# Attention: reciprocal ahead of the next maximum; ctx's output product, norm and queries moved into the opening of the first expert layer

## The reference, cut to what matters

```python
for l in range(DEPTH):
    h = modulate(rms_norm(x, norm1_g[l]), mod[0], mod[1])       # hc the same, of xc
    y, yc = mixer(h, hc)                                        # yc in layer 0 alone
    x = x + mod[2] * y
    h2 = modulate(rms_norm(x, norm2_g[l]), mod[3], mod[4])
    x = x + mod[5] * peer_ffn(h2, ...)
    # layer 0: the same three lines for xc, with modc
# layer 0: yc = concat([attend(qc, kc, vc), conformer_conv(cuc, ...)]) @ w_out
# peer_ffn, for each head: s = q @ sub_keys; the 16 best of 16 + 16; e = their experts
#   act = gelu(sum(x * u[e])); y += softmax(top)[e] * act * v[e]
```

## Time and profile before

| | |
|---|---|
| median of 3 executions | 2536.29 us |
| the profiled execution | 2532.21 us, of which the span of the trace is 2530.2 us |
| busy in the span | PE 77%, DVE 66%, ACT 46%, POOL 35% |
| gathers | 768 (512 in layer 0, 256 in layer 1), 128 rows of 8 KB each: 1.049 MB |
| DMA over the span | 952.22 MB, mean 376 GB/s |
| granted TensorE clock, mean | 0.862 of 2.4 GHz |

### The profile page before, as it was taken

How to read it: one execution, slowest core, us unless ns; L and a number is a source line. 1 busy time by engine, 2 the same in 40 slices (tenths; PEclk the granted TensorE clock), 3 DMA queues, 4 the chain that set the end, 5 groups by cost and what they waited for, 6 DMA issues and landing times. The chain is left out here.

```text
span 2530.2 us, 31698 instructions
## 1 busy us (share of the span) xinstructions
PE 1956.2 (77%) x10844; PEld 935.4 (37%) x10844; DVE 1671.2 (66%) x4157; ACT 1159.4 (46%) x3156; POOL 891.4 (35%) x808
## 2 busy tenths in 40 slices
PE   8999877888786767777877776799997776666765
PEld 5667432443341212333333331478752221122110
DVE  1634589887667667767576867473557666666665
ACT  2342456776635444544453544412335444444444
POOL 0001334544334444444344444100114444444442
PEclk9989898888898878888989998899998877788675
DMA  9554999999999999999999999895169999999997
GB/s 369 206 192 131 411 424 418 422 403 409 425 425 427 426 425 426 426 425 426 422 416 426 426 426 427 295 373 175 73 247 412 426 426 427 426 426 427 427 427 308
DMA packets 146418, 952.22 MB, mean 376 GB/s; under 512 B 16464, under 2 KB 22096, under 8 KB 44752
## 3 DMA queue, kind: packets, MB, share of 16 engines
q0 software_dynamic: 113472, 847.30, 80.2%
q1 hardware_dynamic: 32784, 102.89, 11.1%
HBM read 949.07 MB, written 1.05 MB: 376 GB/s over the span
## 5 line engine op out<-in xcount | busy, mean ns | idle before, releaser
L1080 PE MATMUL pY<-uv,diag 64*64 64x512 f32 x6144 | 992.5, 740 | 504.7 <-ACT diag L1156 485.7
L961 POOL DMA_INDIRECT uv<-uv_dram,idx x768 | 866.5, 1128 | 1270.8 <-PE pY L1080 1027.3
L1314 DVE SCALAR_TENSOR_TENSOR uv<-uv,H 128x1024 f32<-128x1024 f32 x768 | 939.7, 1224 | 535.3 <-DMA uv<-uv_dram,idx 520.6
L1080 PEld LDWEIGHTS pY<-uv,diag 64*64 64x64 f32 x6144 | 194.2, 151 | 1132.9 <-ACT diag L1156 990.2
L1148 ACT ACTIVATE gelu<-dots 128x1 f32<-128x1 f32 x768 | 154.8, 202 | 859.4 <-DVE uv L1314 839.7
L1156 ACT ACTIVATE diag<-cst,coef 128x128 f32<-128x128 f32 x768 | 308.3, 401 | 72.1 <-ACT coef L1152 1.9
L1152 ACT ACTIVATE coef<-gelu,gate 128x1 f32<-128x1 f32 x768 | 226.3, 295 | 28.1 <-issue 0.4
L984 PE MATMUL pqs<-hT,wring 128*128 128x256 f32 x512 | 126.8, 404 | 0.7 <-ACT S L1131 0.7
L984 PEld LDWEIGHTS pqs<-hT,wring 128*128 128x128 f32 x512 | 100.6, 202 | 45.3 <-issue 31.5
L134 PE MATMUL plh<-hT,wring 128*128 128x256 f32 (+1 forms) x512 | 106.3, 368 | 3.7 <-PEq L78 3.3
L1148 ACT ACT_TABLE_LOAD x79 | 101.4, 1283 | 1.4
(11 more groups left out here) (448 smaller groups left out, 2225.3 us busy)
## 6 DMA issues: line engine op xcount, KB each, us to landing
aw<-ada_w_dram POOLq DMA_DIRECT2D x12, 2048.0 KB, 9.6
wring<-peer_q_dram SPq DMA_DIRECT2D x36, 512.0 KB, 13.5
uv<-uv_dram,idx POOLq DMA_INDIRECT x768
wring<-hg_zz_dram SPq DMA_DIRECT2D x20, 512.0 KB, 4.9
wring<-w_in_dram SPq DMA_DIRECT2D x16, 512.0 KB, 10.1
arena<-hg_zz_dram SPq DMA_DIRECT2D x16, 512.0 KB
arena<-ada_w_dram POOLq DMA_DIRECT2D x4, 2048.0 KB
h_aw<-ada_w_dram POOLq DMA_DIRECT2D x4, 2048.0 KB
```

The costliest lines, as they stand in the source:

```text
L961: nc.gpsimd.indirect_dma_start(out=uv[:, n % SLOTS, :], out_offset=None, in_=t[f"uv{l}"], in_offset=bass.IndirectOffsetOnAxis(ap=idx[:, s ...
L1080: last = nc.tensor.matmul(pY[crossed(own, half), b, half * 512:(half + 1) * 512], diag[own, n % DIAGS, own], uv[own, n % SLOTS, D + half * ...
L1314: v.scalar_tensor_tensor(out=uv[:, j, 0:D], in0=uv[:, j, 0:D], scalar=1.0, in1=H2[:, own, :], op0=ALU.mult, op1=ALU.mult, accum_out=dots[: ...
```

## The change

Four edits that belong together.

1. In the context attention, DVE takes the reciprocal of unit u-2 ahead of the maximum of u, not behind the taps; of the taps, 3 lie beside an even unit and 9 beside an odd one (6 and 6 before).
2. The front phase ends after the attention, the convolution and the modulation groups: group 14 moves to loop step u = 16, group 15 behind the transposes of the attention's output. The product with `w_out`, the residual, the norm and the affine of the context leave it. The ring has four w_out tiles, not eight.
3. The opening of `peer_phase(0)` is `ContextOutput`: for block 0 (128 tokens) output product, norm, queries, scores and `topk(0)`; three of block 1's product tiles beside the norm, the rest beside the selection; block 1's norm and queries after it. `topk(1)` and `topk(2)` move beside the picks of step 0, two parts for each pick, and head 1's queries ahead of picks 1 and 3. The last four w_out tiles are loaded into gather buffers 6 and 7 at the phase's start, and gather 6 waits for `b1_out`.
4. The target's first two weight loads (`rest_load`, into `H2`) are issued when block 1's sum of squares is done, ahead of `weights(2)` and `weights(3)`.

```diff
@@ -99,7 +99,7 @@
...
-        lin = [("w_in", 12), ("w_in", 4), ("w_out", 8), ("peer_q0", 16), ("peer_q0", 16),
+        lin = [("w_in", 12), ("w_in", 4), ("w_out", RING), ("peer_q0", 16), ("peer_q0", 16),
@@ -338,9 +342,7 @@
...
-            for i in range(KT):
-                load_tile(sp, "w_out", i, first[2] + i)
-            lin_ahead(sp, 2)
+            lin_ahead(sp, 1)
@@ -511,7 +507,7 @@
...
-                if u < len(UNITS) and u % 2 == 0:
+                if u % 2 == 0:
                     modulate(6 + u // 2)
@@ -534,24 +530,9 @@
...
-            for i in range(2):
-                tile(2, i, range(4))
-            for i in range(2, 4):
-                tile(2, i, range(4))
-            for i in range(4):
-                tile(2, i, range(4, KT))
-            for i in range(4, KT):
-                tile(2, i, whole)
-            for k in range(KT):
-                if k == 6:
-                    modulate(14)
-                pe.wait_ge(r_sq, k + 1)
-                last = mm(A[0][:, 0:T], ones[:], h1[:, k, :], start=(k == 0), stop=(k == KT - 1))
-            last.then_inc(r_sum, 1)
             modulate(15)
             turn(14)
             turn(15)
-            keep_warm(nc, po[:], cst, 4)
@@ -662,7 +643,7 @@
...
-                if u < len(UNITS) and u % 2 == 1:
+                if u % 2 == 1:
                     take_rows(6 + u // 2)
@@ -676,22 +657,11 @@
...
+            take_rows(15)
...
-            act.wait_ge(acc_ready, first[2])
-            for k in range(KT):
-                act.wait_ge(r_out, k + 1)
-                a.activation(h1[:, k, :], xT[:, k, CX], ACT.Square).then_inc(r_sq, 1)
-            take_rows(14)
-            act.wait_ge(r_rs, 1)
-            a.activation(rs[:, XX], rs[:, XX], ACT.Sqrt).then_inc(r_root, 1)
-            take_rows(15)
-            act.wait_ge(m_fin, 5)
-            for k in range(0, KT, 2):
-                act.wait_ge(r_y, k + 1)
-                a.activation(hT[:, k, CX], hT[:, k, CX], ACT.Identity, scale=gainT[:, 0, 1, k, 1:2], bias=modT[:, 0, 3, k, 1:2])
@@ -709,6 +679,7 @@
...
+            TAPS_BESIDE = (3, 9)
@@ -761,19 +732,19 @@
                                        in1=lat_rs[:, k // 2, :], op0=ALU.mult, op1=ALU.mult).then_inc(l_rs, 1)
             taps(60)
             for u in range(len(UNITS) + 2):
+                if u >= 2:
+                    w = u - 2
+                    dve.wait_ge(at["exp"], w + 1)
+                    if w >= 2:
+                        dve.wait_ge(at["norm"], w - 1)
+                    v.reciprocal(mx[:, 6 + w % 2:7 + w % 2], mx[:, 4 + w % 2:5 + w % 2]).then_inc(at["rd"], 1)
                 if u < len(UNITS):
                     x = u % 2
                     dve.wait_ge(at["s"], u + 1)
                     if u >= 2:
                         dve.wait_ge(at["nmx"], u - 1)
                     v.reduce_max(mx[:, x:x + 1], A[x][:, 0:T], AX).then_inc(at["mx"], 1)
-                    taps(6)
-                if u >= 2:
-                    w = u - 2
-                    dve.wait_ge(at["exp"], w + 1)
-                    if w >= 2:
-                        dve.wait_ge(at["norm"], w - 1)
-                    v.reciprocal(mx[:, 6 + w % 2:7 + w % 2], mx[:, 4 + w % 2:5 + w % 2]).then_inc(at["rd"], 1)
+                    taps(TAPS_BESIDE[x])
@@ -782,39 +753,14 @@
...
-            dve.wait_ge(m_turned, 14)
-            dve.wait_ge(at["norm"], len(UNITS))
-            mod_finish(fin, 0, (2, 3, 4, 5), pc[:, 32:96].rearrange("p (n c) -> p n c", c=2))
             dve.wait_ge(c_root, 1)
             v.reciprocal(rs[:, CX], rs[:, CX]).then_inc(c_step, 1)
...
-            def outputs(p):
-
...
-            for p in range(4):
-                outputs(p)
-            dve.wait_ge(r_sum, 1)
-            v.tensor_scalar(rs[:, XX], A[0][:, 0:T], 1.0 / D, EPS, ALU.mult, ALU.add).then_inc(r_rs, 1)
...
-            dve.wait_ge(r_y, KT)
-            for k in range(1, KT, 2):
-                own = hT[:, k, CX]
-                v.tensor_scalar(own, own, gainT[:, 0, 1, k, 1:2], modT[:, 0, 3, k, 1:2], ALU.mult, ALU.add)
             dve.wait_ge(m_turned, GROUPS)
+            mod_finish(fin, 0, (2, 3, 4, 5), pc[:, 32:96].rearrange("p (n c) -> p n c", c=2))
@@ -920,15 +858,15 @@
...
+            opening.sync_late(sp)
...
+            opening.sync_queries(sp)
+            if l == 0:
+                sides[0].sync_first(sp)
@@ -953,7 +891,7 @@
...
-                if opening and n == SLOTS - 2:
+                if n == SLOTS - 2:
                     pool.wait_ge(opening.b1_out, 1)
@@ -1006,59 +944,19 @@
...
+            opening.tensor(pe)
             pe.wait_ge(rows_copied, 2 * BLOCKS)
-            keep_warm(nc, pY[:, 1, 0:512], cst, 9 if l == 0 else 3)
+            keep_warm(nc, pY[:, 1, 0:512], cst, 3)
...
-                if opening and n in (1, 3):
+                if n in (1, 3):
                     queries(1, n // 2)
-                if opening and n == 6:
+                if n == 6:
...
+                if n == 6:
...
-                    if (b, k) == ((1, 2) if late else (0, 9 if opening and s == 0 else 4)):
+                    if (b, k) == ((1, 2) if late else (0, 9 if s == 0 else 4)):
                         queries(h + HEADS_AHEAD, 0)
@@ -1288,13 +1160,10 @@
...
+            opening.vector(dve)
+            for part in range(TOPK):
+                topk(0, part)
+            opening.second(dve)
             inverse(0)
             gates(0)
@@ -1828,6 +1697,225 @@
...
+class ContextOutput:
+
+    BESIDE = 3
...
+    def bank(self, n):
+
+        return self.pY[:, n % 4 // 2, n % 2 * 512 + n // 4 * P:n % 2 * 512 + (n // 4 + 1) * P]
+
+    def sync_late(self, sp):
+
+        for i in range(RING, KT):
+            sp.dma_start(self.late[:, i - RING, :], self.t["w_out"][i]).then_inc(self.late_loaded, 16)
+
+    def sync_queries(self, sp):
+
+        for i in range(RING):
+            self.load_tile(sp, "peer_q0", i, self.q_first + i)
...
+        def products(b, tiles):
+
+            for i in tiles:
+                n, g = KT * b + i, self.out_first + i
+                if i < RING:
+                    pe.wait_ge(self.w_loaded[g % RING], 16 * (g // RING + 1))
+                    w = self.wring[:, g % RING, :]
+                else:
+                    pe.wait_ge(self.late_loaded, 16 * RING)
+                    w = self.late[:, i - RING, :]
+                if n >= 4:
+                    pe.wait_ge(self.x, n - 3)
+                for k in range(KT):
+                    last = mm(self.bank(n), w[:, k * P:(k + 1) * P], self.mixc[:, k, self.cols(b)], start=(k == 0), stop=(k == KT - 1))
+                last.then_inc(self.product, 1)
+                if b == 1 and i < RING:
+                    pe.wait_ge(self.product, n + 1)
+                    pe.sem_inc(self.acc_ready, 1)
+            if b == 1 and KT - 1 in tiles:
+                pe.wait_ge(self.product, 2 * KT)
+                pe.sem_inc(self.b1_out, 1)
...
+        def sums(b):
+
+            for k in range(KT):
+                pe.wait_ge(self.squared, KT * b + k + 1)
+                last = mm(self.b[b][:, 0:P], self.ones[:], self.sq[b][:, k, :], start=(k == 0), stop=(k == KT - 1))
+            last.then_inc(self.summed, 1)
...
+        def rows(b):
+
+            if b == 0:
+                pe.wait_ge(self.x, 2 * KT)
+            for k in range(KT):
+                last = nc.tensor.transpose(self.pY[:, b, k * P:(k + 1) * P], self.hT[:, k, self.cols(b)], self.ident)
+            last.then_inc(self.t_done, 1)
+
+        products(0, range(KT))
+        sums(0)
+        products(1, range(self.BESIDE))
+        queries(0, self.pq)
+        scores(0)
+        products(1, range(self.BESIDE, KT))
+        rows(0)
+        sums(1)
+        queries(1, self.pt)
+        rows(1)
+        scores(1)
+
...
+        affine(0)
+        queries(0, self.pq[:, :, 0:P])
+        scores(0)
+        act.wait_ge(self.table, 1)
+        squares(1)
+        rows(0)
+        exponentials(0)
+        root(1)
+        affine(1)
+        queries(1, self.pt)
+        rows(1)
+        scores(1)
...
+    def vector(self, dve):
+
+        self.residual(dve, 0, range(KT))
+        self.norm(dve, 0)
+        self.residual(dve, 1, range(self.BESIDE))
+
+    def second(self, dve):
+
+        self.residual(dve, 1, range(self.BESIDE, KT))
+        dve.wait_ge(self.x, 2 * KT)
+        dve.sem_inc(self.acc_free, RING)
...
+    def sync_first(self, sp):
+
+        sp.wait_ge(self.opening.summed, 2)
+        for i in range(2):
+            self.rest_load(sp, i)
```

More of the change, by code:

```diff
@@ L405, in tile @@
                         pe.wait_ge(n_ha, 4 + k + 1)
[L406 to L411, removed]
+                    rhs = (h1[:, k, :], Kx[:, k, :])[seq]
                     last = mm(pl[g // 2 % 2][:, i % 2, :], wring[:, g % RING, k * P:(k + 1) * P], rhs,
-                              start=(k == 0 and (i % 2 == 0 or not (seq == 2 and i < 4))), stop=(k == KT - 1),
-                              skip_group_check=True)
```

(59 more changed lines are left out.)

180 lines of the change are left out of this document (110 added, 70 removed).

## The result

| | before | after |
|---|---|---|
| median of 5 executions | 2534.53 us | 2522.59 us |
| ratio, 95% interval | | 0.9945 (0.993 to 0.9961) |
| the profiled execution, span of its trace | 2532.2 us, 2530.2 | 2522.6 us, 2520.8 |
| gather 0 starts | 243.71 | 213.00 |
| mean GB/s in the 100 us from gather 0 | 403 | 372 |

A forecast was written before the change was run, and what follows sets the result against it. Gathers run at the DMA ceiling, so gather 0's start bounds the front. 14 us from the attention and 16 from the half-width opening bring it 30.1 earlier; less 1.5, 2536.3 - 28.6 = 2507.7 us, range 2502 to 2512, wider 2501 to 2517.

The forecast's parts named there:

- its 14 us: Context attention: reciprocal ahead of the maximum shortens four pairs of units from 40.88 to 26.8 us, gain 14, bounds 9.5 and 14.5.
- dips of the clock: Rival, attention: PE's lower-clock dips stay, gain 10 in place of 14, time 2511.7 us; chance 0.13.
- its 15.0 where 1.5 stood: Opening, block 0's output product: 64 matmuls take 15.0 us, plus 1.5 for the pause ahead of it, up to 3.
- that rival: Block 1's norm: a drain at two table switches puts gather 8 off by 2.8 us more, time 2510.5; chance 0.02.
- part 4: After gather 0: picks leave one or two gathers queued; between 0.5 us more filled and 6 more idle, 1.5 taken.
- change nothing at the end: all lie beside gathers: Earlier H2 loads, reordered head-1 queries and layer 1's later modulation were claimed to cost nothing at the end.
- the second rival: Opening at the lower clock: half of block 0's product and queries slow, gather 0 8 us later, 2516; chance 0.08.
- the third, the picks starve the gathers: After gather 0: gather 8 later, PE full from pick 1 to 40, 5 to 8 us idle, 2511 to 2515; chance 0.09.
- The announced sign: Prediction wrong if gather 0 lies past 220 or the window behind it falls under 385 GB/s; 395 to 405 expected.

The follow-up runs named there:

- the tiles ahead: Changed kernel with the target's w_in tiles 2 and 3 loaded behind the first two, 4 to 7 at least eight picks ahead, not four: 2509.72 us, again 2508.14.
- a pause of 7.99 us: Against the tiles ahead: nine 512-column matmuls added on PE ahead of tile 2 at pick 11; 2512.48 us, ratio to before 0.9913.

## Why the prediction was wrong, point by point

- **Direction and start: right.** The attention gives about its 14 us (edit 1 alone: 12.5 at gather 0, 15.2 by the medians), with no dips of the clock. Gather 0 was worked out at 213.6; the three traces of the changed kernel have it at 213.0, 214.6 and 216.0. The product took 2.2 us over its 15.0 where 1.5 stood, all in its first half. The table switch in block 1's norm reads `ACT_TABLE_LOAD` 1.28 us at 219.53 and its activation at 220.83, so the rule weighed in the prediction (the Trainium skill, "ScalarE: Activation LUTs", section "What ACT_TABLE_LOAD costs") has no drain to show here either, and that rival is out.
- **The step that failed is part 4**, "I take 1.5", the term for what comes back after gather 0, between 0.5 us more filled and 6 more idle. It measured 12.3 us in the profiled execution by gather 100 (8.5 and 12.1 in the other two traces; 9.3 to 10.1 in all three by gather 80). Its layout was right: gather 12 was at +36.6 where +36 was worked out, gather 16 at +46.3 where +45 was. It said itself that the engines would then run with one or two gathers queued. What was missing was any wait of PE behind gather 16.
- **Why it was missing.** A side tile was priced by its matmuls alone, and its load as so many bytes. The only landing time that was read was that of loads on quiet queues, 3.6 to 4.1 us; none was read beside running gathers and behind other loads. There the same 512 KB took 18.2 us, and the mixer asks four picks ahead: 10 us at 2.46 each, 8.4 at PE's 2.1. The sentence on the earlier loads, the moved queries and the modulation, "change nothing at the end: all lie beside gathers", was the error in words: it asks whether the DMA engines have room, and not whether PE will wait. The trace of before had the sign. Its first tile landed late too, and PE stood longer than in after:

```profile
268.87 2.08 PE L1924 MATMUL side<-arena,H 128*128 128x256 f32 x4 [9.21 <-DMA H<-w_in_dram]
```

  It cost nothing there (1.4 us lost in gathers 10 to 20), because before had picked 0 to 2 within 16 us of gather 0 and gathers 8 to 10 stood in the queue. In the new order these picks are done only at +29, and the wait that hurts, now the one for the third tile, comes at +53 to +59. What decides is the reserve, the work already given to the DMA engines when PE stops (at 259.66 before, at 266.11 after). How long they stay full, and what they move then:

```profile
259.66:281.66 22.00, 12.79 (x54) 7.27 (x55) 11.60 (x29) 6.11 (x21) 5.00 (x4) 0.69 1.01 425
281.66:289.66 8.00, 8.00 (x49) 3.25 (x47) 5.20 (x14) 3.26 (x8) 3.80 (x4) 1.00 0.94 354
```
```profile
266.11:276.11 10.00, 4.04 (x13) 1.60 (x13) 6.37 (x14) 7.31 (x17) 1.76 (x1) 0.69 1.01 423
276.11:286.11 10.00, 10.00 (x53) 5.94 (x53) 5.23 (x17) 4.85 (x14) 3.68 (x3) 0.96 0.58 193
```

  They stay at the ceiling for 22 us in before (one gather, issued at 273.16, came in between) and for 10 in after. The shorter wait meets the smaller reserve, and is dear.
- **The second term** was the 5 us without work on PE while block 1 is normed: the second rival names these 5 us but prices the lower clock for block 0 alone, and part 4 has no term for it. It cost block 1's queries 2.4 us, which with a late tile behind them became 4.3 us of time.
- **The rival that came true** is the third, the picks starve the gathers, with its place right, its mechanism (low clock) a half, and its price, 5 to 8 us idle, too small. The announced sign held: a window under 385 GB/s was named as what would make the prediction wrong, and it was 372.
- **The sum with the step mended** is 2509.72 and 2508.14 us, where 2507.7 stood. That is not the kernel that was predicted, but against before beside it the gain is 25.8 and 26.6 us where 28.6 stood, so the other terms add up to within 3 us. Of the 12 to 15 us that were missing, some 10 are the late tiles together with the clock. The rest, 2 to 5 us, is a gather 0 that came 0.7 to 2.4 us later than worked out in six of the ten traces with this start, and losses behind gather 80 and between the layers. These differ between traces of one kernel by more than they matter (lead at the last gather 8.5, 17.2 and 9.8 us) and stay open. That edit 1 alone gave 2520.28 and all four 2519.59 beside it says the same from the other side: as it stands the new opening brings next to nothing, and with the tiles ahead another 10.6.

## What to carry to other kernels

When work is moved closer to running gathers, price each load that it waits for by its landing there, with what stands ahead of it in its own queue, and not by bytes or by loads on quiet queues. Both tiles that came late were issued within 5 us behind the query tiles of the next head; the others, asked for just as many picks ahead, came in time. Ask of each wait of the old trace not how long it is but how much reserve stands in front of it: a stop of 9.2 us was free where the DMA engines stayed full for 22 us, and a pause of 7.99 us where they stayed full for 10 cost 5.9 us of DMA time. An expected idle stretch of PE has a second price, the lower clock of the work that follows it.

## What was not expected of the hardware

One 512 KB load took 3.6 to 4.1 us from issue to landing with little else in flight, and 18.2 us when it was issued at 253.81. That is near the 19.7 us that eight gathers take, but eight gathers were not in flight: POOL had issued gather 13 at 251.67, and by 253.81 their queue had moved 13.08 MB, 12.5 of the fourteen gathers of 1.049 MB issued by then. What stood ahead of the load was in its own queue: a `keys` tile of 128 KB and two query tiles of 512 KB, issued from 252.48 on. They landed 8.9, 11.7 and 15.0 us after their issue, at 261.4, 264.6 and 268.3, the tile at 272.0 and the next one at 275.7: one after another, 3.7 us apart. From 260 to 270 us the two queues, gathers (q0) and loads (q1), show packets, MB and share of the engines:

```profile
q0 software_dynamic: 375, 2.80, 66.6%
q1 hardware_dynamic: 394, 1.41, 34.5%
```

Nearly as many packets went through the one as through the other, those of the loads about half as large, so beside running gathers the loads got a third of the bytes: 141 GB/s, and 512 KB in 3.7 us. In the 4.5 us behind the first of these issues the load queue moved only 0.03 MB beside 1.48 MB of gathers; no run shows why. With the tiles ahead the eight loads landed in 8.1 to 17.3 us:

```profile
DMA to landing us min/median/max: 8.1/12.5/17.3
```

So T1's words, that a late tile stands behind queued gathers, fit only the first part of its way. That its own queue makes it late is read from the landings; no run changed that order alone. And after 5.58 us without work PE's granted clock was 0.50, the 1.2 GHz level, in the window from 223 to 228 us; in the kernel with 5.35 us of matmuls in the same place it was 1.00 in the window from 226 to 231 us.
